# The sum of squares of an attention head in one matmul instead of two

## The reference

```python
sc = (jnp.einsum('bqhd,bkhd->bhqk', qn_b, k_nope) + jnp.einsum('bqhr,bkr->bhqk', qr_b, k_rope))
w = jax.nn.softmax(sc * scale, axis=-1)
o = jnp.einsum('bhqk,bkhd->bqhd', w.astype(v.dtype), v)
...
mix = jnp.concatenate([group_rms_norm(attn, g_attn_out[i], N_HEADS),      # y * rsqrt(mean(y * y) + EPS) * g
                       group_rms_norm(conv, g_conv_out[i], CONV_GROUPS)], axis=-1)
```

## Time and profile before

| | |
|---|---|
| time, median of 3 runs | 2714.26 us (2713.51 to 2714.64) |
| the profiled execution's span | 2712.5 us |
| TensorE busy | 2698.8 us, 99% |
| VectorE busy | 2034.9 us, 75% |
| ScalarE busy | 1398.9 us, 52% |
| GpSimd busy | 302.7 us, 11% |
| HBM | 75 GB/s over the span |

### The profile page before, as it was taken

One profiled execution on the slowest core, in us unless ns is written; L12 is line 12 of the kernel. 1 busy time (PEld: TensorE's weight loads), 2 busy tenths in 40 slices (PEclk: granted clock), 3 DMA queues, 4 the chain that ended last, 5 costly groups with the idle time before them and its releaser, 6 DMA issues.

```text
span 2712.5 us, 34671 instructions
## 1 busy us (share of the span) xinstructions
PE 2698.8 (99%) x12854; PEld 2242.9 (83%) x12854; DVE 2034.9 (75%) x2758; ACT 1398.9 (52%) x2401; POOL 302.7 (11%) x329
## 2 busy tenths in 40 slices
PE   9999999999999999999999999999999999999999
PEld 7888888888888888888888888888888888888886
DVE  5468888476787777798866788893867787777986
ACT  5337888564333333356634478884633333333464
POOL 0230000001111111110003200000011111111000
PEclk9999999999999999999999999999999999999999
DMA  4221112531111111133232111133311111111422
GB/s 166 78 72 37 34 34 76 181 109 71 62 47 55 39 58 51 63 117 117 86 119 73 60 41 34 29 132 131 140 45 49 63 47 55 39 55 55 148 94 78
DMA packets 85943, 206.19 MB, mean 76 GB/s; under 512 B 8976, under 2 KB 37776, under 8 KB 84752
## 3 DMA queue, kind: packets, MB, share of 16 engines
q1 hardware_dynamic: 85776, 203.97, 22.3%
HBM read 172.42 MB, written 31.52 MB: 75 GB/s over the span
## 4 chain that ended last, share of the span: by engine, by line
PE 96%; DVE 2%; ACT 1%; DMA 0%; issue 0%; SPq 0%; ACTq 0%
PE ps L1135 28%; PE ps L1137 28%; PE ps L1136 28%; PE ps L1344 4%; PE ps L1369 2%; PE ps L1368 2%; DVE nm L2386 1%; PE ps L1174 0%; PE ps L1175 0%; DVE ptl L2393 0%; PE ps L1309 0%; PE ps L1202 0%; ACT hh L1653 0%; DVE wl L2147 0%; PE ps L1160 0%; PE ps L1161 0%
## 5 line engine op out<-in xcount | busy, mean ns | idle before, releaser
L1135 PE MATMUL ps<-hh,wh 128*128 128x512 f32 x2160 | 847.9, 393 | 1.4 <-DVE hl L2183 1.3
L1137 PE MATMUL ps<-hh,wl 128*128 128x512 f32 x2160 | 840.8, 389 | 0.0
L1136 PE MATMUL ps<-hl,wh 128*128 128x512 f32 x2160 | 840.7, 389 | 0.0
L1653 ACT ACTIVATE wh<-raw 128x256 fp32r<-128x256 f32 (+2 forms) x510 | 319.2, 631 | 443.2 <-PE ps L1137 314.5
L2147 DVE TENSOR_TENSOR wl<-raw,wh 128x256 fp32r<-128x256 f32 (+2 forms) x510 | 379.6, 757 | 159.0 <-ACT wh L1653 158.6
L1135 PEld LDWEIGHTS ps<-hh,wh 128*128 128x128 f32 x2160 | 405.6, 188 | 89.1 <-issue 3.6
L1136 PEld LDWEIGHTS ps<-hl,wh 128*128 128x128 f32 x2160 | 405.6, 188 | 86.9 <-issue 3.6
L1137 PEld LDWEIGHTS ps<-hh,wl 128*128 128x128 f32 x2160 | 405.5, 188 | 84.5
L2574 DVE TENSOR_TENSOR xf<-xf,ps 128x1024 f32<-128x1024 f32 x280 | 337.4, 1214 | 35.9 <-PE ps L1137 34.7
L1135 PE MATMUL ps<-hx,wh 128*128 128x512 f32 x448 | 174.4, 389 | 0.5 <-DVE xf L2574 0.5
L1137 PE MATMUL ps<-hx,wl 128*128 128x512 f32 x448 | 174.3, 389 | 0.0
(11 more groups left out here) (241 smaller groups left out, 4303.3 us busy)
## 6 DMA issues: line engine op xcount, KB each, us to landing
raw<-w_units SPq DMA_DIRECT2D x170, 512.0 KB, 3.4
raw<-w_units SPq DMA_DIRECT2D x112, 256.0 KB, 2.9
x_mid<-xf SPq DMA_DIRECT2D x4, 2048.0 KB, 7.9
xf<-x_mid SPq DMA_DIRECT2D x4, 2048.0 KB, 7.7
hh<-mix_hi SPq DMA_DIRECT2D x14, 512.0 KB, 6.1
hl<-mix_lo SPq DMA_DIRECT2D x14, 512.0 KB, 7.0
stage<-w_head SPq DMA_DIRECT2D x16, 320.0 KB, 3.3
mix_hi<-cyh SPq DMA_DIRECT2D x8, 512.0 KB, 2.6
```

What stands on the lines that cost most here:

```text
L1135: nc.tensor.matmul(dst, ah, bh, start=start, stop=False)
L1136: nc.tensor.matmul(dst, ah, bl, start=False, stop=False)
L1137: return nc.tensor.matmul(dst, al, bh, start=False, stop=stop)
L1653: return nc.scalar.activation(dst, src, ACT.Copy, **more)
```

## The change

The high part of the squares now takes 64 partitions of one 128x512 tile, and the low part the other 64 of the same tile. One matmul by a full matrix of ones sums both. The row of denominators has no partition of its own any more, so it is added beforehand to one of the 64 rows of squares: SyncE fetches it into one partition of the second half of `sq`, and GpSimd adds it there (`add_sums`, 1x512). The high part waits for this addition. The square is now written to the 64 partitions where the high part will stand. In the hand-written lists the steps `sq_high` and `sq_low` move to later places; `ATT_PE` is as it was.

```diff
--- before.py
+++ after.py
@@ -222,16 +222,16 @@
 
 ATT_ACT = steps("""
 high.0.0.0 high.0.0.1 exp.0.1 y.-1.0 v.1.0 k.1.0 last.7.1 exp.0.2 high.0.1.0 high.0.1.1 exp.0.3 v.1.1 k.1.1
-out.-1.1 high.0.2.0 high.0.2.1 square.-1.1 sq_high.-1.1 unit.0 last.6.0 high.0.3.0 high.0.3.1 exp.0.4 ln.-1.1
+out.-1.1 high.0.2.0 high.0.2.1 square.-1.1 unit.0 last.6.0 high.0.3.0 sq_high.-1.1 high.0.3.1 exp.0.4 ln.-1.1
 last.7.2 exp.0.5 v_turned.1 high.0.4.0 high.0.4.1 r.-1.1 q.1.0 exp.0.6 y.-1.1 high.0.5.0 high.0.5.1 exp.0.7
-out.0.0 high.0.6.0 high.0.6.1 square.0.0 last.7.3 sq_high.0.0 q.1.1 high.0.7.0 high.0.7.1 exp.1.0 ln.0.0 r.0.0
+out.0.0 high.0.6.0 high.0.6.1 square.0.0 last.7.3 q.1.1 sq_high.0.0 high.0.7.0 high.0.7.1 exp.1.0 ln.0.0 r.0.0
 """)
 
 ATT_DVE = steps("""
 scale.-1.0 low.0.0.0 low.0.0.1 least.0.2 k.1.0 last.7.1 least.0.3 low.0.1.0 low.0.1.1 y.-1.0 k.1.1 sum.-1.1
-low.0.2.0 low.0.2.1 sq_low.-1.1 least.0.4 low.0.3.0 low.0.3.1 den.0.0 least.0.5 unit.0 last.6.0 last.7.2
+low.0.2.0 low.0.2.1 least.0.4 low.0.3.0 sq_low.-1.1 low.0.3.1 den.0.0 least.0.5 unit.0 last.6.0 last.7.2
 v_turned.1 least.0.6 q.1.0 low.0.4.0 low.0.4.1 scale.-1.1 least.0.7 q_low.1.0 low.0.5.0 low.0.5.1 q.1.1
-sum.0.0 low.0.6.0 low.0.6.1 den.0.1 last.7.3 sq_low.0.0 least.1.0 q_low.1.1 low.0.7.0 low.0.7.1 y.-1.1
+sum.0.0 low.0.6.0 low.0.6.1 den.0.1 last.7.3 least.1.0 q_low.1.1 sq_low.0.0 low.0.7.0 low.0.7.1 y.-1.1
 least.1.1
 """)
 
@@ -682,6 +682,7 @@
         den_turn = sem("den_turn")
         den_out = sem("den_out")
         den_in = sem("den_in")
+        den_add = sem("den_add")
         o_var = sem("o_var")
         o_ln = sem("o_ln")
         o_r = sem("o_r")
@@ -870,9 +871,15 @@
         def low_at(h, a, t):
             return yl[rows(a), :] if h < HEADS - 2 else hl[rows(a), PAIRS - 1, hs(t)]
 
-        def square_parts(h):
-
-            return (wh[:, 1, 0:4, :], wl[:, 1, 0:4, :]) if h < HEADS - 1 else (yh[:, :], yl[:, :])
+        def square_part(h, low):
+
+            part = rows(h % 2 if low else 1 - h % 2)
+            return half_of(wh, 1)[part, 0, :] if h < HEADS - 1 else yh[part, :]
+
+        def sum_row(h, i):
+
+            first = V_DIM * (1 - h % 2)
+            return sq[first:first + 1, i, :]
 
         def is_kr(w):
             return w < O_AT and kind_of(w)[0] == "kr"
@@ -1069,9 +1076,11 @@
 
                     O = (L * HEADS + h) * 2 + t
                     sp.wait_ge(den_out, 64 * O + 64)
-                    if O:
-                        sp.wait_ge(o_ln, O)
-                    sp.dma_start(sq[rows(1 - h % 2), 0, :], sums[O:O + 1].partition_broadcast(V_DIM)).then_inc(den_in, 16)
+                    if t:
+                        sp.wait_ge(den_add, O)
+                    elif O:
+                        sp.wait_ge(o_y, O)
+                    sp.dma_start(sum_row(h, 1), sums[O:O + 1]).then_inc(den_in, 16)
 
                 def load_mix(c, done):
                     sp.dma_start(hh[:, c, :].bitcast(f32), mix_hi[c]).then_inc(done, 16)
@@ -1374,7 +1383,8 @@
 
                     O = (L * HEADS + h) * 2 + t
                     pe.wait_ge(o_sq_lo, O + 1)
-                    two_passes(ps[:, 6 + t, :], ones_r[:, 2 + a, :], *square_parts(h)).then_inc(o_var, 1)
+                    parts = half_of(wh, 1)[:, 0, :] if h < HEADS - 1 else yh[:, :]
+                    nc.tensor.matmul(ps[:, 6 + t, :], ones_r[:, 0, :], parts, start=True, stop=True).then_inc(o_var, 1)
 
                 def mix_part(n, order, start, stop):
 
@@ -1892,17 +1902,17 @@
 
                     O = (L * HEADS + h) * 2 + t
                     act.wait_ge(o_sum, O + 1)
-                    nc.scalar.activation(sq[rows(a), 0, :], of[rows(a), :], ACT.Square).then_inc(o_sq, 1)
+                    nc.scalar.activation(sq[rows(1 - a), 0, :], of[rows(a), :], ACT.Square).then_inc(o_sq, 1)
 
                 def high_of_squares(h, t):
                     O = (L * HEADS + h) * 2 + t
                     act.wait_ge(o_sq, O + 1)
-                    act.wait_ge(den_in, 16 * O + 16)
+                    act.wait_ge(den_add, O + 1)
                     if (h, t) == (0, 0):
                         act.wait_ge(in_out, (L + 1) * len(IN_OUTS))
                     if (h, t) == (HEADS - 1, 0):
                         act.wait_ge(mix_stored, (L + 1) * MIX_STORED)
-                    copy(square_parts(h)[0], sq[:, 0, :]).then_inc(o_sq_hi, 1)
+                    copy(square_part(h, 0), sq[rows(1 - h % 2), 0, :]).then_inc(o_sq_hi, 1)
 
                 def output_ln(h, a, t):
                     O = (L * HEADS + h) * 2 + t
@@ -2409,8 +2419,7 @@
                 def low_of_squares(h, t):
 
                     dve.wait_ge(o_sq_hi, (L * HEADS + h) * 2 + t + 1)
-                    high, rest = square_parts(h)
-                    low(rest, sq[:, 0, :], high).then_inc(o_sq_lo, 1)
+                    low(square_part(h, 1), sq[rows(1 - h % 2), 0, :], square_part(h, 0)).then_inc(o_sq_lo, 1)
 
                 def output(h, a, t, j):
 
@@ -2672,14 +2681,28 @@
                 pool.wait_ge(lr_lo, L * 10 + 10)
                 nc.gpsimd.tensor_tensor(carry[:, :], eps[:, :], eps[:, :], ALU.add)
                 nc.gpsimd.memset(vv[:, :, :, 0:V_DIM].bitcast(f32), 0.0).then_inc(v_zero, 1)
+
+                def add_sums(h, t):
+
+                    O = (L * HEADS + h) * 2 + t
+                    pool.wait_ge(den_in, 16 * O + 16)
+                    pool.wait_ge(o_sq, O + 1)
+                    pool.wait_ge(den_sq, min(O + 2, (L + 1) * HEADS * 2))
+                    nc.gpsimd.tensor_tensor(sum_row(h, 0), sum_row(h, 0), sum_row(h, 1), ALU.add).then_inc(den_add, 1)
+
                 for h in range(HEADS):
                     for t in range(2):
                         O = (L * HEADS + h) * 2 + t
                         pool.wait_ge(s_exp, step(L, h, 4 * t + 3) + 1)
                         if O >= 2:
                             pool.wait_ge(den_turn, O - 1)
+                            pool.wait_ge(den_add, O - 1)
                         part = den[:, h % 2, 4 * t:4 * t + 4]
                         nc.gpsimd.tensor_tensor(den2[:, t, 0:4], part, part, ALU.mult).then_inc(den_sq, 1)
+                        if h or t:
+                            add_sums(*((h, 0) if t else (h - 1, 1)))
+                add_sums(HEADS - 1, 1)
+                pool.wait_ge(den_add, (L + 1) * HEADS * 2)
 
                 pool.wait_ge(x_new, post_at(L, 0) * 16 + 16)
                 nc.gpsimd.tensor_tensor(carry[:, :], eps[:, :], eps[:, :], ALU.add)
```

## The result

| | before | after |
|---|---|---|
| median of the runs, us | 2714.31 | 2753.46 (2753.28 to 2757.09) |
| ratio, 95% interval | | 1.0149 [1.0137, 1.016] |
| span of the profiled execution, us | 2712.5 | 2751.6 |
| TensorE busy, us | 2698.8 | 2709.5 |

The change makes the kernel 39.1 us slower. The forecast was 2737 (+23) with a range of 2723 to 2742: the sign is right, the forecast is 16 us too low, and the time is outside the range.

The account below looks back on a forecast made before the run. TensorE, busy 2698.8 of 2712.5 us, was taken as the bound. Per layer, stops 8.4, half 1 -1.6, head 7 -0.2 and the factor's hold 5.0 make 11.6; two layers +23.2, so 2737 us, range 2723 to 2742.

Parts of the forecast that it names:

- The stop at half 0: Heads 0 to 6: TensorE waits at the single matmul for VectorE's moved low part, 14 times, at least 1.5 us each.
- 2.1 to 2.4 (held): Microseconds of each TensorE wait at half 0's matmul if GpSimd's addition delays VectorE's factor; otherwise 1.5 to 1.7.
- half 1 of heads 0 to 6: Low part ends in time, by 0.1 us at the least; each saves 0.23 us, seven times a layer.
- The held factor: VectorE's multiplication of denominators (0.18 us) waits for GpSimd's addition to end, 0.65 or 0.75 us a head, 5.0 a layer.
- The clock: TensorE's granted clock was read as 1.00 (2.4 GHz) in the heads; no term for a fall after a stop.
- 1.74 us of standing still: TensorE's stop at half 0 of an odd head, before any hold; 1.51 us net of the 0.23 matmul.
- Head 6: TensorE's idle time there, 0.92 and 0.34 us, absorbs 1.26 of the stop's 1.28 us net loss, leaving 0.02.
- given back in part: VectorE and ScalarE run ahead while TensorE stands, recovering part of the stops: +3 to +9 us; chance 0.07.
- the forecast without the hold: Rival: VectorE's factor of the denominators isn't delayed by GpSimd's addition; +13.2 us, 2727.5 us; chance 0.31.

Follow-up runs that it names:

- the experiment: Changed kernel with the constant of the denominators multiplied in by GpSimd, so VectorE only transposes: 2726.65 us, ratio 1.0048.
- the filled one: Changed kernel with eight 128x512 matmuls whose result nobody reads, put ahead of half 0's matmul in heads 0 to 6: 2739.32 us, ratio 1.0094.
- the one with three matmuls in the stop: Changed kernel with three matmuls whose result nobody reads, in place of eight, ahead of half 0's matmul: 2739.65 us, ratio 1.0095.
- order-alone: Kernel before with only sq_high and sq_low moved in ScalarE's and VectorE's lists, two matmuls, no GpSimd addition: 2733.49 us, ratio 1.0074.
- the old order: Changed kernel with sq_high and sq_low back at their old places in ScalarE's and VectorE's lists: 2757.46 us, ratio 1.0161.

## Why the prediction was right in sign and too low

*The stop at half 0: right.* 14 stops, at the single matmul, for VectorE's low part, 13 of them of 2.08 to 2.11 us where "2.1 to 2.4 (held)" was named, and none at half 1 of heads 0 to 6, where the matmul stands 0.3 to 0.5 us behind the low part's end. At the stops that end reaches TensorE after 0.06 us, where 0.14 was taken. The addition takes 1.28 us (1.29 was taken from the first row). The Trainium skill (GPSIMD Engine Reference, section 1) gives each core its own 16 partitions; by that one partition is no cheaper than 128, and the rows agree: 1.28 for 1x512, 1.29 for 128x512.

*The held factor: right, and nearly in size.* 10.0 us were forecast. The changed kernel's VectorE groups (instruction, tiles, count | busy us, mean ns of one | idle time before it) have

```profile
L2413 DVE TENSOR_SCALAR dent<-dent 128x32 f32<-128x32 f32 x32 | 16.7, 523 | 1.1
```

and 32 by 0.18 is 5.8, so the factors are 10.9 us longer than they would be. 15 of 32 are held, at 0.75 us in odd heads and 1.00 to 1.03 in even ones and head 7: the 13 ahead of the stops of 2.1 us, which make 9.2 of the 10.9, and two in head 7. The 12.7 us of the experiment hold the instruction itself too, which that kernel takes off VectorE (some 0.1 us of distance in 14 halves); the rest of the difference, about 2 us, is open. The one stop of 1.40 us is the counter-proof inside the same run. In order of time, half 0 of head 2, layer 1:

```profile
324.19 0.18 DVE L2413 TENSOR_SCALAR dent<-dent 128x32 f32<-128x32 f32 x1
324.22 1.28 POOL L2691 TENSOR_TENSOR sq<-sq 1x512 f32<-1x512 f32 x1 [2.58 <-ACT sq L1905]
...
327.00 0.50 PE L1387 MATMUL ps<-wh,ones_r 128*128 128x512 f32 x1 [1.40 <-DVE wh L2157]
```

The factor came 0.03 us ahead of the addition, took its 0.18, and the stop is 0.7 us shorter. So who comes first decides. That is what the Trainium skill says of VectorE's operations in a two-port mode or with two inputs in SBUF (SBUF — State Buffer, "SBUF: two separate sides": an exclusive lock, against the one that came first), and the rows agree for a one-input operation with a constant, which no row of before showed. The mode itself is in no row; that the factor has one was inferred from its pace.

*The clock: the step that failed.* The prediction made a stop cost its own length, "1.74 us of standing still", and read the 1.00 of the earlier trace rows as given. Behind nine of the stops the granted clock was 0.50 for 3.4 us. The cost is 14.1 us (changed kernel less the filled one), priced at nothing and named in no rival. It makes up most of the 16 us that were missing. No row of before could give the price, but the trace could have told of the risk: its granted clock of 1.00 in the heads goes with waits of TensorE of 0.5 us at most. For a stop four times as long, which that trace doesn't hold, the prediction needed a low and a high price of the clock, as it had two ends for the factor.

*Head 6: failed too, a small one.* "They take up 1.26 of head 6's 1.28" did not happen. The matmul of head 6's half 0 is 15.13 us late in layer 1 (473.38 against 458.25), the last of the layer 16.58 (516.16 against 499.58): between them 1.45 more, of which 1.54 is a spell. Without it that is -0.1, where -1.85 was predicted (the layer's 11.6 less 13.45 up to head 6: the 1.26, and the matmuls saved). In layer 2 the late start grows by 21.15 us up to head 6 and by 1.47 from there, the same picture. The kernels without spells agree: from -0.05 to -0.14 us in this stretch in the filled ones and in the one without the factor. TensorE's idle time there, which was to be used up, is still there: 0.45, 0.21 and 0.52 us in three waits, 1.18 in all, in place of 1.27. VectorE, which was to be that stretch's own bound, waits for TensorE instead. Order of time, VectorE, head 6, first in the changed kernel, then in the one with three matmuls in the stop (before, the same minima start at 461.57 without a wait):

```profile
477.78 1.23 DVE L2396 TENSOR_REDUCE nm<-ps 128x1 f32<-128x1024 f32 x1 [2.41 <-PE ps L1146]
```

```profile
473.18 1.23 DVE L2400 TENSOR_REDUCE nm<-ps 128x1 f32<-128x1024 f32 x1 [0.90 <-PE ps L1146]
```

In the changed kernel TensorE was at the lower clock there (474.3 to 477.7), which makes the wait longer. But the second row has it at a clock of 1.00: the scores come late by the stop itself, everything behind them moves with them, and so do the waits. The two layers so lose 3.5 us more than forecast.

*The sum by places.* Forecast +23.2; nine spells by 1.54, +13.9; heads 6 and 7 of both layers, +3.5 (twice -0.1 for -1.85); the stops of layer 1 a little shorter than forecast (the one of 1.40 and the first, which shifts TensorE by 1.87 for 2.26), -1.4. That is +39.2.

*The rival "given back in part"* has some truth in the order: without factor the stops are 1.05 and 1.29 us where 1.51 and 1.74 were worked out. Yet the time of that kernel is +12.6, and the forecast without the hold was +13.2. That near hit is luck, since two misses cancelled: shorter stops, and no gain in head 6.

*Open:* why a stop of 2.1 us is followed by a lower clock in nine of 13 cases and not in all, with their places changing from one execution to the next. The stops of up to 1.42 us in the changed kernel, the order-alone and the three-matmul one never were. That is no sure bound: in the kernel with the old order, which stands twice in a head, spells followed three of the stops of 1.53 and 1.54 us (granted clock 0.50 from 458.6 to 462.0 behind the stop that ended at 457.15), and none followed its stops of 1.74 and 1.76 us. So the length of a stop alone doesn't decide.

## What to carry to other kernels

Where TensorE is full and every other engine nearly so, an operation that is taken off TensorE but lengthens the chain to its inputs is worth its saving only if the chain has the slack; here it had 0.0 to 0.2 us and got 1.3 of addition. Price a stop of TensorE with three terms: its length, what the waiting order holds elsewhere (a VectorE instruction that meets a GpSimd one), and the granted clock behind it, for which a clock measured while the engine never stood long is no evidence. To split such a cost, fill the stop with work that nobody reads: if the kernel gets faster by that, it was the clock.

## What the runs showed of the hardware

- A stop of TensorE of 2.1 us in an otherwise full stream was followed by 3.4 us at 1.2 GHz in nine of 13 cases (18 of 26 over two executions), 1.54 us each or a little more; the places changed between the executions; three of eight 128x512 matmuls in the stop were enough to avoid all of them, -13.8 us.
- A VectorE operation of 0.18 us on 128x32, one input and a constant, took 0.75 to 1.03 us when it came into a GpSimd operation on one single partition. A 128x32 transposition (0.20 us) in the same addition did not become longer, nor did reads from PSUM (20 minima that started inside an addition, 1.21 to 1.22 us).
- An addition of 1x512 takes GpSimd 1.28 us, one of 128x512 takes it 1.29 us.
